# A second group of turns and value products is placed inside the next half's score rows, and GpSimd rounds keys and queries, in a fused decoder step on one Trainium2 core

## The reference

```python
s = jnp.einsum('bqhd,bkhd->bhqk', qb, k).astype(jnp.float32) * scale
s = s + jnp.swapaxes(cqb, 1, 2)[..., None] - ck[:, :, None, :]
s = jnp.where(kpos[None, :] <= qpos[:, None], s, NEG_INF)
p = jax.nn.softmax(s, axis=-1)
return jnp.einsum('bhqk,bkhd->bqhd', p.astype(v.dtype), v)
```

## Time and profile before

| what | value |
|---|---|
| median of 3 runs (1900.69 to 1908.21) | 1904.42 us |
| the profiled execution's own time | 1904.6 us |
| its span, first to last instruction | 1902.6 us |
| PE busy | 1721.6 us, 90% |
| DVE, ACT, POOL busy | 867.0, 674.3 and 321.1 us |
| chain that ended last, PE's share | 74% |

### The profile page before, as it was taken

The page is one execution under the profiler, slowest core; times in us unless marked ns, Lnnn a source line. Parts: engine busy times, 40 slices in busy tenths (PEclk is TensorE's granted clock), DMA queues, the critical chain, the costliest instruction groups (busy, mean ns, idle before and its releaser), DMA issues.

```text
span 1902.6 us, 31400 instructions
## 1 busy us (share of the span) xinstructions
PE 1721.6 (90%) x11034; PEld 1584.1 (83%) x11034; DVE 867.0 (46%) x1361; ACT 674.3 (35%) x1094; POOL 321.1 (17%) x335
## 2 busy tenths in 40 slices
PE   6999999999999859999999999999865888899997
PEld 5999999999989759888888888888643555598997
DVE  4433333343253484555565555555543333423443
ACT  5111111111053233555655556565531232302322
POOL 4111111100000021322222122222121222000110
PEclk8999999999999879999999999999866999899998
DMA  4111111111201203211101021110235799821102
GB/s 142 46 46 45 46 44 45 44 36 44 76 28 44 88 19 93 58 46 35 57 23 59 21 79 45 34 57 24 68 144 173 281 373 362 303 68 41 42 28 94
DMA packets 165110, 161.87 MB, mean 85 GB/s; under 512 B 19661, under 2 KB 141661, under 8 KB 164935
## 3 DMA queue, kind: packets, MB, share of 16 engines
q1 hardware_dynamic: 154566, 126.38, 21.0%
q0 software_dynamic: 10496, 34.88, 5.0%
HBM read 137.41 MB, written 23.81 MB: 85 GB/s over the span
## 4 chain that ended last, share of the span: by engine, by line
PE 74%; DVE 9%; issue 5%; ACT 5%; DVEq 2%; DMA 2%; ACTq 1%; SPq 1%; POOL 1%; POOLq 0%
PE PS L620 14%; PE PS L622 14%; PE PS L621 14%; PE PS L781 4%; PE PS L782 4%; PE PS L783 4%; PE PS L840 3%; PE PS L887 3%; PE PS L828 2%; PE PS L939 2%; PE PS L811 2%; DVE small L1522 2%; DVE pTl L1533 2%; PE PS L812 1%; PE PS L908 1%
## 5 line engine op out<-in xcount | busy, mean ns | idle before, releaser
L620 PE MATMUL PS<-Hhi,w_hi 128*128 128x364 f32 (+1 forms) x1536 | 513.1, 334 | 36.2 <-DVE Hlo L1367 32.9
L622 PE MATMUL PS<-Hhi,w_lo 128*128 128x364 f32 (+1 forms) x1536 | 510.7, 333 | 0.0
L621 PE MATMUL PS<-Hlo,w_hi 128*128 128x364 f32 (+1 forms) x1536 | 510.3, 332 | 0.0
L620 PEld LDWEIGHTS PS<-Hhi,w_hi 128*128 128x128 f32 x1536 | 294.9, 192 | 41.1 <-issue 29.1
L621 PEld LDWEIGHTS PS<-Hlo,w_hi 128*128 128x128 f32 x1536 | 295.0, 192 | 0.0
L622 PEld LDWEIGHTS PS<-Hhi,w_lo 128*128 128x128 f32 x1536 | 294.2, 192 | 0.0
L781 PE MATMUL PS<-Hhi,w_hi 128*128 128x364 f32 (+1 forms) x768 | 274.6, 358 | 0.1
L782 PE MATMUL PS<-Hlo,w_hi 128*128 128x364 f32 (+1 forms) x768 | 252.6, 329 | 0.0
L783 PE MATMUL PS<-Hhi,w_lo 128*128 128x364 f32 (+1 forms) x768 | 252.6, 329 | 0.0
L505 POOL TENSOR_TENSOR w_raw<-w_raw,GT 128x1024 f32<-128x1024 f32 x65 | 127.1, 1956 | 697.2 <-DMA w_raw<-in_w_kv 385.6
L1014 ACT ACTIVATE w_hi<-w_raw 128x1024 fp32r<-128x1024 f32 (+1 forms) x97 | 105.5, 1089 | 371.2 <-PE PS L622 368.5
(11 more groups left out here) (247 smaller groups left out, 2207.3 us busy)
## 6 DMA issues: line engine op xcount, KB each, us to landing
Kpages<-in_cache_k SPq DMA_DIRECT2D x64, 512.0 KB, 7.0
Vpages<-in_cache_v POOLq DMA_DIRECT2D x64, 512.0 KB, 9.8
w_raw<-in_w_in_a SPq DMA_DIRECT2D x64, 256.0 KB, 3.0
w_raw<-in_w_ple_gate SPq DMA_DIRECT2D x16, 512.0 KB, 3.7
w_raw<-in_w_kv SPq DMA_DIRECT2D x32, 256.0 KB, 3.2
w_raw<-in_w_in_b SPq DMA_DIRECT2D x32, 256.0 KB, 3.4
parked_x<-X SPq DMA_DIRECT2D x8, 544.0 KB, 5.2
X<-parked_x SPq DMA_DIRECT2D x8, 544.0 KB, 7.5
```

The lines of the kernel that those rows point to most:

```text
L620: mm(out, wh, hi[:, k, s:e], start=(k == 0), stop=False)
L621: mm(out, wh, lo[:, k, s:e], start=False, stop=False)
L622: last = mm(out, wl, hi[:, k, s:e], start=False, stop=(k == nk - 1))
```

## The change

Group 1 of a half no longer runs at the half's end. Its turns and value products become the steps ("B", ...), which stand between the score rows 1 to 6 of the next half, and ("B", "O") puts its output on DVE behind the maximum of row 6, the seventh. The first half has none, and after the last half the list `BEHIND` does what is left. Group 0 comes later, with 9 dense pieces at the end of the half. The rounding of keys and queries moves from ACT to POOL, with a drain between its copies: the first head's keys behind the odd half's first four normalisations, the others behind its last one. The emptying of z moves to p = 21, 22 and 23, the split of the values to 21 and 23, and the store of a pair to the next even half, behind the second load.

```diff
-STEPS = [("S", 0), ("D", 2), ("N", 0), ("N", 1), ("D", 1), ("S", 1), ("D", 2), ("N", 2), ("D", 1), ("S", 2), ("D", 3),
-         ("S", 3), ("D", 3), ("S", 4), ("D", 4), ("T", 0, 0), ("T", 0, 1), ("S", 5), ("D", 5), ("V", 0, 0), ("T", 0, 2),
-         ("S", 6), ("D", 6), ("V", 0, 1), ("T", 0, 3), ("S", 7), ("D", 6), ("V", 0, 2), ("D", 1), ("V", 0, 3), ("D", 5),
-         ("T", 1, 0), ("T", 1, 1)]
+STEPS = [("S", 0), ("D", 2), ("N", 0), ("N", 1), ("D", 1), ("S", 1), ("D", 1), ("N", 2), ("D", 2), ("B", "T", 0), ("B", "T", 1),
+         ("S", 2), ("D", 2), ("B", "V", 0), ("B", "T", 2), ("D", 1), ("B", "V", 1), ("B", "T", 3),
+         ("S", 3), ("D", 2), ("B", "V", 2), ("B", "T", 4), ("D", 2), ("B", "V", 3), ("B", "T", 5),
+         ("S", 4), ("D", 2), ("B", "V", 4), ("B", "T", 6), ("D", 2), ("B", "V", 5), ("B", "T", 7),
+         ("S", 5), ("D", 2), ("B", "V", 6), ("D", 1), ("B", "V", 7), ("D", 2),
+         ("S", 6), ("B", "O"), ("D", 3), ("T", 0), ("T", 1), ("D", 2), ("S", 7), ("D", 2), ("R",), ("D", 1), ("V", 0), ("T", 2),
+         ("D", 3), ("V", 1), ("T", 3), ("D", 3), ("V", 2), ("D", 3), ("V", 3), ("D", 9)]
+BEHIND = [("B", "T", 0), ("B", "T", 1)]
 for _kb in range(8):
-    STEPS += [("D", 1 if _kb < 7 else 2), ("V", 1, _kb)] + ([("T", 1, _kb + 2)] if _kb < 6 else [])
+    BEHIND += [("B", "V", _kb)] + ([("B", "T", _kb + 2)] if _kb < 6 else [])
+BEHIND += [("B", "O")]
...
+            def store_y(j):
+                sp.wait_ge(sems["o_done"], START["o_done"] + 4 * j + 4)
+                sp.sem_inc(sems["sp_step"], 1)
+                sp.dma_start(d["y"][bass.ds(j, 1)].rearrange("a p n -> (a p) n"), yT[:, 0:SEQ]).then_inc(sems["y_out"], 16)
...
+                if more:
                     load_b1(j, 2, 1)
                     sp.wait_ge(sems["score"], START["score"] + 16 * j + 8)
                     sp.sem_inc(sems["sp_step"], 1)
...
+            def k_hi(j, hh):
+                g.wait_ge(sems["staged"], 3 * j + 4)
+                if not (isinstance(j, int) and j < 0) and hh == 1:
+                    g.wait_ge(sems["score"], START["score"] + 16 * j + 16)
+                g.sem_inc(sems["pool_step"], 1)
+                for half in range(2):
+                    g.drain()
+                    g.tensor_copy(KA[64 * half:64 * half + 64, hh, :], stK[64 * hh:64 * hh + 64, 0:SEQ])
+                g.drain().then_inc(sems["kq_hi"], 1)
+            def q_hi(j, hh):
+                g.wait_ge(sems["staged"], 3 * j + 5)
+                g.sem_inc(sems["pool_step"], 1)
+                g.drain()
+                g.tensor_copy(QA[64 * hh:64 * hh + 64, hh, :], stQ[64 * hh:64 * hh + 64, 0:SEQ])
+                g.drain()
+                g.tensor_copy(QB[0:HD, hh, :], stQ[64 * hh:64 * hh + 64, 0:SEQ])
+                g.drain().then_inc(sems["kq_hi"], 1)
...
                         normalise(8 * hh + qb, j)
                         if not more and hh == 1:
                             early_values(2 * qb)
+                    if more and hh == 1:
+                        k_hi(j, 0)
                     if more:
                         gain_b1(j, (1, 3)[hh], 1)
                     for qb in range(4, 8):
@@ -566,12 +602,19 @@
                             early_values(2 * qb)
                     if more and hh == 0:
                         gain_b1(j, 2, 1)
+                if more:
+                    q_hi(j, 0)
+                    k_hi(j, 1)
+                    q_hi(j, 1)
...
+            def behind(prev, step, banks):
+                if step[1] == "T":
+                    turn_p(*prev, 1, step[2], banks if step[2] == 0 else None)
+                elif step[1] == "V":
+                    pv_step(*prev, 1, step[2])
...
                     if step[0] == "V":
-                        pv_step(j, half, step[1], step[2])
+                        pv_step(j, half, 0, step[1])
+                    if step[0] == "B" and prev is not None:
+                        behind(prev, step, kept)
                     if step[0] == "N" and (half == 0 or more):
                         turn_part(j + half, 1 - half, step[1])
...
+                half_pair(j, 1, True, (j, 0))
+                half_pair(j + 1, 0, True, (j, 1))
+            half_pair(NPAIR - 2, 1, True, (NPAIR - 2, 0))
+            half_pair(NPAIR - 1, 0, False, (NPAIR - 2, 1))
+            half_pair(NPAIR - 1, 1, False, (NPAIR - 1, 0))
+            for step in BEHIND:
+                behind((NPAIR - 1, 1), step, None)
             pe.wait_ge(sems["act_evac"], EA_B2)
...
                     act.drain().then_inc(sems["staged"], 1)
-                if i == 2:
-                    q_hi(0, 0)
-                    q_hi(0, 1)
...
-            leaves = [{7: (0, 0), 15: (0, 1), 23: (0, 2), 31: (1, 0), 39: (1, 1), 47: (1, 2)},
+            leaves = [{21: (0, 0), 22: (0, 1), 23: (0, 2), 31: (1, 0), 39: (1, 1), 47: (1, 2)},
                       {7: (2, 0), 15: (2, 1), 23: (2, 2), 45: (3, 0), 46: (3, 1), 47: (3, 2)}]
...
                     w_hi((N_B1 + i) % 2, B_B1 + 3 * (4 * j + 3 + i), gained=32 + 4 * j + 3 + i + 3)
-                if half == 0 and p == 4 and attend:
+                if half == 0 and p == 21 and attend:
                     act.wait_ge(sems["kv_nat"], 6 * j + 6)
                     act.wait_ge(sems["pv"], START["pv"] + 24 * j)
                     af(VS[:, :, :, 0:HD], KN[:, 0:8, :].rearrange("p t (h n) -> p t h n", h=2), ACT.Copy).then_inc(sems["v_hi"], 1)
-                if half == 1 and p in (7, 10) and more:
-                    k_hi(0, (7, 10).index(p))
-                if half == 1 and p == 28 and attend:
-                    act.wait_ge(sems["score"], START["score"] + 16 * j + 16)
-                if half == 1 and p in (28, 35) and more:
-                    k_hi(1, (28, 35).index(p))
-                if half == 1 and p in (10, 35) and more:
-                    act.drain().then_inc(sems["kq_hi"], 1)
-                if half == 1 and p in (40, 43) and more:
...
                     w_lo((N_B1 + i) % 2, N_B1 + 4 * j + 3 + i + 1)
-                if half == 0 and p == 6 and attend:
+                if half == 0 and p == 23 and attend:
...
+            def behind(prev, step):
+                if step[1] == "T":
+                    p_lo(*prev, 1, step[2])
+                elif step[1] == "O":
+                    output(*prev, 1)
...
+                    if step[0] == "R":
+                        row_sum(j, half, 7)
                     if step[0] == "T":
-                        p_lo(j, half, step[1], step[2])
...
+                    if step[0] == "V" and step[1] == 3:
+                        output(j, half, 0)
+                    if step[0] == "B" and prev is not None:
+                        behind(prev, step)
                     if step[0] == "D":
                         for _ in range(step[1]):
                             beside(j, half, p, True, more)
-                            if p == 29:
-                                row_sum(j, half, 7)
                             p += 1
```

More of the change, by code:

```diff
@@ L398, in half0 @@
                     load_b1(j, 1, 1)
+                if not first:
+                    store_y(j - 1)
+                if more:
                     load_b1(j, 2, 1)
@@ L574, in _ @@
                 gain_b1(0, t)
+            for hh in range(2):
+                k_hi(-1, hh)
+                q_hi(-1, hh)
             with g.Fori(0, NPAIR - 1) as j:
@@ L849, in half_pair @@
                     if step[0] == "T":
-                        turn_p(j, half, step[1], step[2], more)
+                        turn_p(j, half, 0, step[1], kept if step[1] == 0 and prev is None else None)
                     if step[0] == "V":
-                        pv_step(j, half, step[1], step[2])
+                        pv_step(j, half, 0, step[1])
+                    if step[0] == "B" and prev is not None:
+                        behind(prev, step, kept)
                     if step[0] == "N" and (half == 0 or more):
@@ L1600, in beside, with behind, half_pair @@
                     ve.drain().then_inc(sems["kq_lo"], 1)
-                if half == 0 and attend and p == 25:
+                if half == 0 and attend and p == 28:
                     ve.wait_ge(sems["z_done"], j + 1)
                     ve.tensor_copy(at_pair(zsS, j).rearrange("p a n -> p (a n)"), zf[:, SEQ:])
-            def half_pair(j, half, more):
+            def behind(prev, step):
+                if step[1] == "T":
+                    p_lo(*prev, 1, step[2])
+                elif step[1] == "O":
+                    output(*prev, 1)
+            def half_pair(j, half, more, prev):
                 p = 0
@@ L1615, in half_pair @@
                         keep_part(j + half, 1 - half, step[1])
+                    if step[0] == "R":
+                        row_sum(j, half, 7)
                     if step[0] == "T":
-                        p_lo(j, half, step[1], step[2])
-                    if step[0] == "V" and step[2] == (3, 7)[step[1]]:
-                        output(j, half, step[1])
```

(5 more changed lines are left out.)

74 lines of the change are left out of this document (37 added, 37 removed).

## The result

The changed kernel takes 1950.67 us (median, 1945.49 to 1953.83); the kernel before, run beside it, 1906.16. The ratio is 1.0235, with a 95% interval of 1.0201 to 1.027. The profiled execution took 1953.23 us, 48.6 more than the one before, with a span of 1951.6.

The account below looks back on a forecast made before the run. TensorE bounds the kernel, so only its waits could be won. The fourteen halves +32.2, last halves +0.5, ahead of the stage +1.5, clock 2.8: +37.0 on 1904.6 gives 1941.6, said as 1941, range 1922 to 1960 (0.55).

Parts of the forecast that it names:

- bank 0 in the even half: Piece 24, even half: PE waits 2.3 for ACT to empty z's first bank, held behind group 1's output.
- silu, at product 0: Even half, group 0's first product: PE waits 0.6, as its pTh stands behind ACT's emptying, table load and silu.
- keys, product 6: Odd half, group 1's block 6: PE waits 2.7 for pTl, queued on DVE behind k_lo, which waits for GpSimd's casts.
- queries, product 2: Odd half, group 0's block 2: PE waits 3.8 behind q_lo and GpSimd's casts; bounds 2.6 and 4.9.
- the half's end, piece 0: Start of the next even half: PE waits 3.0 behind GpSimd's last casts and DVE's rests; bounds 1.0 and 3.3.
- clock, all halves: TensorE at 1.2 GHz for at least 3.4 us behind the queries' wait: net 0.4 a pair, 2.8 in all.
- up to the last group's turns: The last two halves, after the fourteen: 67.5 us where it was 67.0, so +0.5.
- ahead of the stage: Before the fourteen halves: GpSimd makes eight casts in a row, +1.5, bounds 0 and 3.
- rival (c): GpSimd's casts take 1.9, as the two-operand gain does: about +6 a pair, 1983; chance 0.07.
- rival (d): The clock falls behind the waits of 2.3 and 2.7 too: about +5 a pair, 1976; chance 0.14.
- Rival (a): GpSimd's detour is mild: waits of 0.9, 2.6 and 1.0, clock stays, 5.4 a pair less, 1903; chance 0.13.
- rival (b): GpSimd's signals come before DVE asks, so nothing of the detour is seen: 10.0 a pair less, 1869; chance 0.11.

Follow-up runs that it names:

- ACT's last version: Changed kernel with ACT rounding, copies, rests, output and silu spaced out, and the next pair's first gain behind the even half's first normalisation: 1862.02 us, ratio 0.9778.
- the experiment with the moved gain: Changed kernel with only GpSimd's gain of the fourth weight tile moved, behind row 5's normalisation in the odd half: 1928.53 us, ratio 1.0125.

## Why the prediction came near, point by point

The forecast for the profiled execution was 1941.6; it took 1953.2, 11.6 more. The direction and the four places were right. The nearness is in part luck: the slow clock cost 37 us more than the term for it, and the halves without waits took 2 more. The waits came out 14 below their terms, the last halves 5.5 below, and the time ahead of and behind the stage 8.3 below.

| term | forecast | measured |
|---|---|---|
| bank 0 in the even half | 2.3 | 2.23 |
| silu, at product 0 | 0.6 | 0.96 in the first half; none in the other even ones |
| keys, product 6 | 2.7 | 2.53 |
| queries, product 2 | 3.8 | 3.6 to 3.9 |
| the half's end, piece 0 | 3.0 ahead of the clock's share | 2.2 in the first half, then 1.7 or 0.6 |
| half without waits | 39.0 | 39.0 even, 39.5 odd |
| first half without waits | 33.7 | 32.6 |
| clock, all halves | 2.8, what it hides at piece 0 taken off | about 40, nothing taken off |
| fourteen halves | 625.6 | 651.0 |
| up to the last group's turns | +0.5 | -5.0 |
| ahead of the stage | +1.5 | -1.9 |
| behind it | 0 | -4.9 |

The halves without waits are read from ACT's last version (40.24 - 1.23, 40.35 - 0.81, 32.6). They give 543.1 for the fourteen, where the forecast had 540.7. The waits in the changed kernel are 67.9 for 82.1. And 651.0 - 543.1 - 67.9 leaves 40 for the clock, for 2.8. The 40 is an estimate, as it takes the halves of another kernel.

**Keys and queries.** Both waits came out within 0.2 us, and the experiment with the moved gain shows the step that was only argued from the earlier trace rows: the two engines exclude each other for whole instructions (the copy of 64 columns lasts until the gain is done), and the one that waits is next (the gain behind `KB`, then the copy behind the gain). SBUF — State Buffer of the Trainium skill (SBUF: two separate sides) states it as an exclusive lock that is held for the whole instruction; the trace agrees, with 1.89 for a 64-column copy and 0.18 where the gain is away. The cast is 1.04, at the 1.0 taken, and ACT's copy of the same form was 1.05. So rival (c) is out, and the duration of the casts is not what cost. GPSIMD Engine Reference of the Trainium skill (Engine selection) puts one input at roughly line rate, and the trace agrees with 1.04 beside ACT's 1.05.

**Bank 0.** Right in size and cause; moving the output alone removes it.

**The silu.** The 0.6 should not have been added to the 2.3. While PE stands at piece 24 and then runs slowly, ACT catches up. So 3.6 us of this term, six times 0.6, were wrong.

**The half's end.** The terms of this step add up to 19.5 and not to the 19.3 that the prediction gives, which would make the wait 3.3 in place of 3.0. The step trusted least held better than its number: with the wait at product 2 taken away the wait at piece 0 is 6.2, where 3.8 and 3.0 make 6.8. What stood there in the changed kernel depends on how much slow clock lies between, 0.6 behind 6.8 us of it and 1.7 behind 3.4.

**The clock is the step that failed.** I took one stretch at 1.2 GHz for a pair, behind the longest wait, and 0.4 net for it. The trace has 22 falls in fourteen halves: behind the wait at product 2 or ahead of its end, behind that at piece 24 in the steady even halves, behind product 6 in most odd halves, and behind the 1.7 at piece 0. That is the mechanism of rival (d), with its 5 a pair, 35 in all; measured are 37 more than the 2.8. The time came out at 1951 and not at the rival's 1976 because six waits at piece 0 add up to 7.9 and not to 18, part of it by that very clock, and because of the terms that came out lower at the stage's ends. The forecast left it at 0.14 because nothing in the stage had shown a wait between 1.8 and 3.2; the bound of 3.2 was the only row with a fall, and I treated the gap as if the limit lay at its upper end. Rival (a) is out by the waits, and rival (b) in two ways: GpSimd's signals were late, and even without them, with ACT rounding, the time is 1901 and not 1869.

**The last halves.** The first of the two took 36.4 for the 38.2 of the forecast, since its wait at piece 0 was 0.5 and not 3.0; the last took 25.6 for 29.3. For that one I took a lone chain of maximum and exponential for each row, with group 1 fitted into it at its own cost. The kernel before has two waits of turns for GpSimd in its last half, and the one of 3.9 stands between rows 4 and 5:

```profile
PE PS L811 <- ACT Pb L1151: 5.9, 4, 2.2
PE PS L828 <- POOL Pb L537: 3.9, 1, 3.9
```

In the changed kernel's the turns and products of group 1 fill these, up to the same point:

```profile
PE PS L854 <- ACT Pb L1208: 3.5, 3, 1.6
PE PS L883 <- DVE pTl L1580: 2.2, 4, 1.0
```

**Ahead of and behind the stage.** It begins 1.9 earlier and pays 2.2 at its first piece 0, together 0.3 where I had 1.5. The 4.9 behind it (4.5 of them within the span) are not explained: from the first turned page of keys to the end the profiled runs of the twelve kernels take 470 (four), 473 (three) or 475 us (five), without relation to what they change; before is of the last kind and after of the first.

## What to carry to other kernels

A copy that moves to an idle engine is not priced by its duration, which was the same here, but by what it stands behind in that engine's queue and by which instructions of DVE read SBUF at that time. The same eight copies a pair cost 50 us more on GpSimd than on ACT, still 30 to 36 with everything placed for them, and one GpSimd instruction moved behind the next two normalisations gave back 22. Several waits within one half may be one chain: take one away and see whether the next grows. And an order that fills gaps paid only once the output, the silu, the copies, the rests and the gain were placed for it. With ACT rounding it gives 0.2%, less than a measurement can tell from no change, as it was first written, and 2.2% with all of these moved.
